# The eight looped up chunks of the first feed-forward half, written out in line in four engines' programs

## The reference

```python
def swiglu(x, w_gate, w_up, w_down):
    return (jax.nn.silu(x @ w_gate) * (x @ w_up)) @ w_down

h = jnp.concatenate([meta, x], axis=1)                       # 528 x 1024
h = h + 0.5 * swiglu(rmsnorm(h, ffn1_norm[l]), ffn1_w_gate[l], ffn1_w_up[l], ffn1_w_down[l])   # D_FF = 2816
u = rmsnorm(h, mix_norm[l])
...                                                          # mixer, second feed-forward, second block
```

## Time and profile before

| what | value |
|---|---|
| median of 3 runs | 1557.88 us (1556.37 to 1559.57) |
| profiled execution: its own time | 1557.85 us |
| profiled execution: span | 1556.2 us |
| PE busy | 1519.9 us, 98% of the span |
| DVE busy | 955.3 us, 61% |
| ACT busy | 593.6 us, 38% |
| instructions recorded | 30392 |

### The profile page before, as it was taken

One profiled execution on the slowest core, in us unless ns is written; L12 is line 12 of the kernel. 1 busy time (PEld: TensorE's weight loads), 2 busy tenths in 40 slices (PEclk: granted clock), 3 DMA queues, 4 the chain that ended last, 5 costly groups with the idle time before them and its releaser, 6 DMA issues.

```text
span 1556.2 us, 30392 instructions
## 1 busy us (share of the span) xinstructions
PE 1519.9 (98%) x12676; PEld 1334.2 (86%) x12676; DVE 955.3 (61%) x1528; ACT 593.6 (38%) x968; POOL 127.0 (8%) x124
## 2 busy tenths in 40 slices
PE   9999999999999989999999989999999989999998
PEld 8999999999997779988888868888888877776777
DVE  6546588855389776546345666634666565557872
ACT  6222356632255562043223312212222143446960
POOL 0000100000001640500000000000000000000410
PEclk9999999999999999999999999999999999999999
DMA  6222223246332200012224243333342353211001
GB/s 242 81 99 75 92 100 109 92 114 145 96 85 70 61 3 31 5 42 81 94 90 166 82 162 127 131 119 123 134 153 76 106 213 135 76 47 55 2 13 71
DMA packets 27679, 147.85 MB, mean 95 GB/s; under 512 B 2928, under 2 KB 3328, under 8 KB 16944
## 3 DMA queue, kind: packets, MB, share of 16 engines
q1 hardware_dynamic: 21616, 122.50, 22.5%
q0 software_dynamic: 5424, 22.68, 5.3%
q10 hardware_dynamic: 528, 1.08, 0.2%
HBM read 140.97 MB, written 5.27 MB: 94 GB/s over the span
## 4 chain that ended last, share of the span: by engine, by line
PE 87%; DVE 7%; ACT 3%; issue 2%; DMA 1%; POOL 1%; DVEq 0%; SPq 0%; ACTq 0%; POOLq 0%
PE PS L745 22%; PE PS L746 22%; PE PS L747 22%; PE PS L845 2%; PE PS L847 2%; PE PS L846 2%; PE PS L1262 1%; PE PS L1197 1%; PE PS L1157 1%; PE PS L1247 1%; PE PS L1260 1%; ACT PB L1900 1%; PE PS L781 1%; DVE WLO L2125 1%; PE PS L1070 1%
## 5 line engine op out<-in xcount | busy, mean ns | idle before, releaser
L1542 ACT ACTIVATE WHI<-RAW 128x2048 fp32r<-128x2048 f32 (+3 forms) x113 | 189.4, 1676 | 276.2 <-PE PS L747 272.4
L2125 DVE TENSOR_TENSOR WLO<-RAW,WHI 128x2048 fp32r<-128x2048 f32 (+3 forms) x113 | 226.0, 2000 | 65.9 <-ACT WHI L1542 65.2
L745 PE MATMUL PS<-UH,WHI 128*128 128x264 f32 (+1 forms) x736 | 226.9, 308 | 2.1 <-DVE WLO L2125 2.1
L746 PE MATMUL PS<-UH,WLO 128*128 128x264 f32 (+1 forms) x736 | 225.7, 307 | 0.0
L747 PE MATMUL PS<-UL,WHI 128*128 128x264 f32 (+1 forms) x736 | 225.4, 306 | 0.0
L745 PE MATMUL PS<-UHS,WHI 128*128 128x512 f32 x520 | 205.6, 395 | 5.5 <-DVE WLO L2125 5.5
L746 PE MATMUL PS<-UHS,WLO 128*128 128x512 f32 x520 | 203.4, 391 | 0.0
L747 PE MATMUL PS<-ULS,WHI 128*128 128x512 f32 x520 | 203.4, 391 | 0.0
L745 PEld LDWEIGHTS PS<-UH,WHI 128*128 128x128 f32 x736 | 138.5, 188 | 9.1 <-DVE WLO L2125 2.5
L746 PEld LDWEIGHTS PS<-UH,WLO 128*128 128x128 f32 x736 | 138.4, 188 | 6.4 <-issue 0.2
L747 PEld LDWEIGHTS PS<-UL,WHI 128*128 128x128 f32 x736 | 138.2, 188 | 6.3
(11 more groups left out here) (474 smaller groups left out, 3241.2 us busy)
## 6 DMA issues: line engine op xcount, KB each, us to landing
RAW<-in_f2u SPq DMA_DIRECT2D x22, 1024.0 KB, 4.8
RAW<-in_f1u SPq DMA_DIRECT2D x21, 1024.0 KB, 4.8
ADA<-in_ada POOLq DMA_DIRECT2D x24, 512.0 KB, 4.7
RAW<-in_f1d SPq DMA_DIRECT2D x16, 704.0 KB, 4.1
RAW<-in_f2d SPq DMA_DIRECT2D x16, 704.0 KB, 4.1
RAW<-in_wi SPq DMA_DIRECT2D x10, 1024.0 KB, 4.8
RAW<-in_w SPq DMA_DIRECT2D x8, 1024.0 KB, 5.4
RAW<-in_mg SPq DMA_DIRECT2D x8, 1024.0 KB, 4.8
```

What stands on the lines that cost most here:

```text
L745: mm(out, WHI[:, slot, c:c + w], hi, start=first, stop=False)
L746: mm(out, WLO[:, slot, c:c + w], hi, start=False, stop=False)
L1542: A(WHI[:, slot, 0:w], RAW[:, slot, 0:w], ACT.Copy).then_inc(hi_rdy, 1)
L2125: TT(WLO[:, slot, 0:w], RAW[:, slot, 0:w], WHI[:, slot, 0:w].bitcast(f32), ALU.subtract).then_inc(lo_rdy, 1)
```

## The change

`stream` gets `straight=True` for `f1u0` on SP, PE, ACT and DVE, where before only `f1u1` (and what was in line already) had it:

```diff
-            stream(sp, name, load(name), straight=name == "f1u1", first=2 if name in ("f1d0", "f1d1") else 0)
+            stream(sp, name, load(name), straight=name in ("f1u0", "f1u1"), first=2 if name in ("f1d0", "f1d1") else 0)
...
-                stream(pe, f"f{f + 1}u{half}", up, straight=f == 0 and half == 1, first=2)
+                stream(pe, f"f{f + 1}u{half}", up, straight=f == 0, first=2)
...
-                stream(act, f"f{f + 1}u{half}", up, straight=f == 0 and half == 1, first=2)
+                stream(act, f"f{f + 1}u{half}", up, straight=f == 0, first=2)
...
-                stream(dve, f"f{f + 1}u{half}", up, straight=f == 0 and half == 1, first=0 if half else 2)
+                stream(dve, f"f{f + 1}u{half}", up, straight=f == 0, first=0 if half else 2)
```

## The result

The changed kernel takes 1568.75 us (median of 20 runs) against 1558.19 us for the kernel before (median of 20 runs): the ratio is 1.0066, with a 95% interval of 1.0054 to 1.0078. It is slower by 10.6 us. The profiled execution took 1568.31 us, with a span of 1566.6 us, 10.4 us longer than before.

What follows compares the result with a forecast made beforehand. The prediction took PE to bound the kernel. To the profiled 1557.85 us it added 0 (PE), 0 (DVE, ACT), 0 (SP), 0.1 (fetching) and 0 (shift), giving 1557.95, predicted as 1557.9 us; range 1555.6 to 1560.2 us.

Steps and rivals of the forecast that it cites:

- direct gain of 0: In the changed loop, PE's removed register, counter and branch instructions were hidden: 0, at most 1.75 us if unhidden.
- rival in which branches back stall the fetch: In the changed loop, taken branches force refetching, so removal gains: 1551.9 to 1554.9 us; 3 in 100.
- rule of the Trainium skill: A taken branch outside the held pages forces a fetch before execution goes on; the change would gain some microseconds.
- covers of DVE, ACT and SP: In the changed stage, low weights 2.8 us early and loads with 2.3 us of room hide these engines' savings: 0.
- sign that I had set for this: The prediction is wrong altogether if a later stage moves by more than 3 us.
- wrong row: PE's idle time at L1171 that no engine explains, 3.2 us in six pieces, was used to price the text shift.
- contention was priced in one direction: In the changed stage, a load losing a packet's 1.0 us would still have 1.3 us of its room left.
- slower rival: In the changed stage, late 16 KB pieces stop PE, at most 1.0 us for each of 5 packets: 1562.9 us; 5 in 100.
- places of lower clock: Behind the stage, one of two short places vanishing or coming anew moves the time 1.5 to 3.4 us; 4 in 100.

Runs made afterwards that it cites:

- e2: The kernel before with SP, ACT and DVE in line while PE keeps its loop: 1558.47 us, ratio 0.9997.
- e10: The changed kernel with SP waiting for `st_rdy` 2 ahead of the `mg` loads, until the inverse stage is over: 1558.96 us, ratio 0.9991.
- e11: The kernel before with SP waiting for `st_rdy` 2 ahead of the `mg` loads: 1558.78 us, ratio 0.9992.
- e1: The kernel before with only PE's eight up chunks in line; SP, ACT and DVE keep their loops: 1570.34 us, ratio 1.0071.
- e3: The kernel before with PE alone changed, four chunks in line ahead of its loop: 1570.67 us, ratio 1.0075.
- e5: The kernel before with SP waiting for `a_ps` 10 ahead of the `mg` loads: 1569.24 us, ratio 1.0064.
- e7: The changed kernel with PE's text padded so that the inverse stage (L1244) begins a 16 KB piece: 1571.41 us, ratio 1.0081.
- e8: The kernel before with PE held up once ahead of L1260 by a semaphore from a 2 KB transfer ACT issues: 1566.74 us, ratio 1.0033.
- e9: The changed kernel with PE's text padded so that L1244 begins 128 instructions into a 16 KB piece: 1559.34 us, ratio 1.0001.

## Why the prediction was wrong

**Right: the changed stage.** The direct gain of 0, taken from a ceiling of 1.75 us, holds: 193 matmuls a window before and after, and the stage as long as before. The rival in which branches back stall the fetch, and with it the rule of the Trainium skill that it was weighed against, is not borne out for PE: without its branches the stage is no shorter (138.30 - 21.39 = 116.91 us against 138.07 - 21.15 = 116.92 us). The covers of DVE, ACT and SP held too, and e2 shows their three lines at a ratio of 0.9997.

**Right: the added text in its own stage.** I expected 88 to 90 packets on q8 and some of them between 57 and 126 us. There are 88, with four in that stretch, and PE isn't stopped by any.

**Wrong: "Behind the stage the program text of PE, DVE and ACT lies shifted ... I bound it at 1 us in either direction and take 0."** This is the step that failed. The text lies 127 instructions past a whole number of pieces, and that moved one request under a load: 0.7 us of pause and 10.8 us of half clock, 11.5 us in place of at most 1. The sign that I had set for this, a later stage that moves by more than 3 us, came true. The bound came from the wrong row. The waits at L1171 are the same 3.2 us in all thirteen kernels, wherever the text lies, so they say nothing about fetching. I should have gone to the stage in which PE uses up its text fastest. There a piece lasts 3.7 us, where in the changed stage it lasts some 15 us, and a 1 MB load holds the DMA engines for 3.5 us of these.

**Wrong: the contention was priced in one direction.** I asked what a packet of text costs a load (1.0 us of 2.3 us of room) and not what a load costs a packet of text. The 1 MB loads keep the engines busy (78.9% and 94.4% in the windows shown) for some 3.5 us at a time; the packet of text waits for that, and PE behind it.

**Wrong in place: the slower rival.** It was the right kind of mechanism, a piece that comes too late, but I put it into the changed stage only, gave it 5 in 100, and priced it at 1.0 us a packet. What it lacked was the clock: a pause under 1 us became a loss of ten. I had priced the places of lower clock as a spread of runs, on the ground that "nothing in the change touches what PE does before either of them". The half clock at 604 us is a new place, and the change does touch what PE does before it. For a new place I had allowed up to 3.4 us, the size of the one near 914 us; this one cost 10.8 us.

## What to carry to other kernels

- A change of program length is not local. Everything behind it is fetched at other moments; compare the fetch queue with the big loads in the stage where an engine goes through its text fastest, and price the meeting from the side of the fetch.
- In a stage of small matmuls, price a pause of PE with what the clock may do behind it, not with its own length. Here a pause of 0.7 us cost 11.5 us with what followed it.
- If a load isn't needed soon, hold it back behind such a stage. Here this cost nothing, and the two places of the text that differed by 10.6 us then took the same time (e10 and e11).

## What the runs showed of the hardware

- PE asks for its text one piece ahead in this stage: in the changed kernel a piece due near 599.1 us was needed for the matmul after 602.63 us, one piece later. A packet that is over at 602.1 us let PE go on at 603.4 us, so some 1.3 us lie between its end and the next matmul (1.2 to 1.4 us in e1, e3, e5 and e7 too).
- A loop of 393 PE instructions, one and a half pieces, ran without any packet on q8 in 57 to 126 us, over two branches back; what had been brought in was used again.
- The stage of 64x64 matmuls ran for more than 20 us at a granted clock of 1.00 without a drop. After one pause of 0.5 to 1.6 us it stood at 0.50 for 20.5 (e3, e8) to 27.3 us (e7), although PE was busy all the time. In all six the `mg` load had ended 0.5 to 1.4 us ahead of the pause. A pause of 1.2 us with no engine behind it near the head of the same stage (e9, at 586.4 us, L1245, 14 us before the load) and one of 1.1 us between its two groups of blocks, for DVE, in the kernel before (618.5 us, 18 us behind the load) had no such effect. What sets these apart, the nearness of a load or something else, was not tested.
